# Compact near products in a diagonal scan, C turned by 128 columns, the first output chunk in other banks, and a new slot table

## The reference, cut to what matters

```
h = rms(x); u, z_s5, q, k, v, z_da = split(h @ e_w_in)
# S5: 64 groups of 16 channels, 64 complex states each; per token l:
x_l = Bbar u_l ; h_l = a * h_(l-1) + x_l ; y_l = Re(C h_l) + d * u_l
y = gelu(y); y = y * sigmoid(y @ w_glu + b_glu) * silu(z_s5)
# differential attention, 8 heads with two score maps each, ALiBi, rms of the output
x = x + concat(y_s5, y_da) @ e_w_out
```

## Time and profile before

| | us |
|---|---|
| median of three runs (lowest, highest) | 985.17 (984.67, 985.78) |
| the profiled execution, time | 983.37 |
| the profiled execution, span of the trace | 981.6 |
| DVE busy / ACT busy in the span | 629.2 / 572.5 |
| ACT splitting weights (L942) / DVE splitting weights (L950) | 310.1 / 361.1 |

### The profile page before, as it was taken

One profiled execution on the slowest core, in us unless ns is written; L12 is line 12 of the kernel. 1 busy time (PEld: TensorE's weight loads), 2 busy tenths in 40 slices (PEclk: granted clock), 3 DMA queues, 4 the chain that ended last, 5 costly groups with the idle time before them and its releaser, 6 DMA issues.

```text
span 981.6 us, 14482 instructions
## 1 busy us (share of the span) xinstructions
PE 966.3 (98%) x5315; PEld 828.8 (84%) x5315; DVE 629.2 (64%) x995; ACT 572.5 (58%) x934; POOL 94.4 (10%) x92
## 2 busy tenths in 40 slices
PE   8999999999999999999999999999999999999998
PEld 7988888788787999888888888888888888888887
DVE  5687898898889755665554654555455545555553
ACT  5697758767567655654445465446545654565332
POOL 2101002011021010000002200220022002200000
PEclk9999999999999999999999999999999999999999
DMA  8874444334433447565799985667999956654662
GB/s 287 207 205 151 151 134 135 119 107 129 141 110 117 129 129 264 166 202 188 173 168 175 168 180 166 177 184 151 173 155 175 196 163 177 180 167 151 215 215 86
DMA packets 113858, 163.63 MB, mean 167 GB/s; under 512 B 19221, under 2 KB 54154, under 8 KB 113546
## 3 DMA queue, kind: packets, MB, share of 16 engines
q1 hardware_dynamic: 99504, 159.67, 61.7%
q10 hardware_dynamic: 14298, 3.22, 1.6%
HBM read 160.76 MB, written 2.10 MB: 166 GB/s over the span
## 4 chain that ended last, share of the span: by engine, by line
PE 90%; DVE 5%; ACT 4%; issue 1%; DMA 0%; SPq 0%; ACTq 0%
PE bank L452 22%; PE bank L454 22%; PE bank L453 22%; PE bank L479 4%; PE bank L480 4%; PE bank L481 4%; ACT uz L1054 2%; PE bank L706 1%; PE bank L691 1%; ACT wh L942 1%; DVE wl L950 1%; PE bank L595 1%; PE bank L520 1%; PE bank L586 1%; PE bank L698 1%
## 5 line engine op out<-in xcount | busy, mean ns | idle before, releaser
L950 DVE TENSOR_TENSOR wl<-raw,wh 128x1024 fp32r<-128x1024 f32 x295 | 361.1, 1228 | 273.0 <-ACT wh L942 271.8
L942 ACT ACTIVATE wh<-raw 128x1024 fp32r<-128x1024 f32 x295 | 310.1, 1057 | 170.0 <-PE bank L454 124.6
L452 PE MATMUL bank<-wh,xh 128*128 128x512 f32 x768 | 309.1, 403 | 0.0
L454 PE MATMUL bank<-wh,xl 128*128 128x512 f32 x768 | 300.3, 391 | 0.0
L453 PE MATMUL bank<-wl,xh 128*128 128x512 f32 x768 | 299.2, 390 | 0.0
L454 PEld LDWEIGHTS bank<-wh,xl 128*128 128x128 f32 x768 | 144.1, 188 | 31.7
L453 PEld LDWEIGHTS bank<-wl,xh 128*128 128x128 f32 x768 | 144.7, 188 | 26.9
L452 PEld LDWEIGHTS bank<-wh,xh 128*128 128x128 f32 x768 | 144.5, 188 | 27.0 <-DVE wl L950 0.2
L452 PE MATMUL bank<-wh,yh 128*128 128x512 f32 x256 | 100.7, 393 | 1.4 <-ACT scr L1345 1.4
L454 PE MATMUL bank<-wh,yl 128*128 128x512 f32 x256 | 99.8, 390 | 0.0
L453 PE MATMUL bank<-wl,yh 128*128 128x512 f32 x256 | 99.6, 389 | 0.0
(11 more groups left out here) (326 smaller groups left out, 1107.2 us busy)
## 6 DMA issues: line engine op xcount, KB each, us to landing
raw<-in_o_w_in SPq DMA_DIRECT2D x128, 512.0 KB
raw<-in_e_w_in SPq DMA_DIRECT2D x130, 256.0 KB, 3.2
raw<-in_e_w_out SPq DMA_DIRECT2D x32, 512.0 KB
raw<-in_o_w_out SPq DMA_DIRECT2D x32, 512.0 KB
raw<-in_e_w_in SPq DMA_DIRECT2D x31, 512.0 KB
raw<-in_s_w_glu SPq DMA_DIRECT2D x8, 512.0 KB
res<-in_x SPq DMA_DIRECT2D x8, 256.0 KB, 6.9
res<-in_x SPq DMA_DIRECT2D x1, 2048.0 KB, 10.1
```

The costliest lines, as they stand in the source:

```text
L452: nc.tensor.matmul(o, l_hi, w_hi, start=first, stop=False)
L454: mm = nc.tensor.matmul(o, l_lo, w_hi, start=False, stop=last)
L942: nc.scalar.activation(wh[:, j % RING, :], raw[:, j % RING, :], ACT.Copy).then_inc(hi_done, 1)
L950: nc.vector.tensor_tensor(wl[:, j % RING, :], raw[:, j % RING, :], wh[:, j % RING, :].bitcast(F32), ALU.subtract).then_inc(lo_done, 1)
```

## The change

Five things change, all in layer 0.

1. **Near products.** DVE no longer writes `ca` with its zeros: it writes the compact C-times-powers into `cc` (8 x 5 x 16 columns, all 128 partitions, one instruction instead of two of 64 partitions). PE multiplies `ba` by the 64 compact columns, and the skip term by 16 columns. ACT spreads the result into `near` with eight scaled copies per call (scale 1 or 0 by row group) instead of four, and a new ACT piece `s5_pad` makes the padded `ca` from `cc` with two copies of 64 partitions for each of the two parts; `s5_out_y` waits for it.
2. **C turned by 128 columns.** C is loaded twice into both halves of `c_n` (six matrix loads on ACT's queue instead of four, in six consecutive slots), PE uses four 128-column transposes per call instead of eight 64 x 64 products, one slot earlier, and ACT's `c_out` becomes four calls of two copies.
3. **First output chunk.** It accumulates in `xb` and `yb`, so it no longer waits for the sigmoids; the second now waits for all eight, the fourth for the second chunk's sum. In each of its units ACT and DVE now do the gate pieces ahead of the split of the weights.
4. **Slots.** Nearly all slots of scan and attention move.
5. **Waits.** `rotate_in` and `rotate_out` wait for the near products and the pad; small setup reductions build `ident16` and `of_group`.

```diff
-TAB_SLOT, FAR_SLOT, BA_SLOT = [-2, -2], [-6, -1], [-11, -2]
-T_SLOT = [0, 0, 0, 0]
-NEAR_SLOT, HOLD_SLOT, SKIP_SLOT = [0, 4], 4, -9
-X_SLOT, YN_SLOT, Y_SLOT = [3, 6], 7, [9, 9]
-IN_SLOT, OUT_SLOT = [4, 8], [5, 8]
+TAB_SLOT, FAR_SLOT, BA_SLOT = [0, 0], [-6, -4], [-8, -2]
+T_SLOT = [-1, -1, -1, -1]
+NEAR_SLOT, HOLD_SLOT, SKIP_SLOT = [-1, 1], 6, -11
+X_SLOT, YN_SLOT, Y_SLOT = [0, 5], 3, [8, 9]
+IN_SLOT, OUT_SLOT = [2, 6], [6, 6]
+PAD_SLOT = [-3, 3]
-QKT_SLOT = [-3, -3]
+QKT_SLOT = [-3, -2]
-PV_SLOT = [5, 7]
-YT_SLOT = [10, 11]
-V_SLOT, SILU_SLOT = 4, 5
-SQUARE_SLOT, SUM_SLOT, NORM_SLOT = [9, 10], [8, 10], [10, 13]
+PV_SLOT = [5, 8]
+YT_SLOT = [8, 13]
+V_SLOT, SILU_SLOT = 3, 6
+SQUARE_SLOT, SUM_SLOT, NORM_SLOT = [8, 10], [8, 9], [11, 11]
...
+        out0_acc = [[xb, yb], acc[1], acc[0], acc[1]]
... PE, s5_near
                 if h == 0:
-                    pe.wait_ge(ca_done, i + 1)
+                    pe.wait_ge(cc_done, 2 * i + 2)
                     pe.wait_ge(dd_done, i + 1)
                 for e in range(TH):
-                    t, at = TH * h + e, e * P
-                    nc.tensor.matmul(o[0:32, at:at + P], ba[:, 0, t, 0:32], ca[:, 0, t, 0:P], start=True, stop=False)
-                    nc.tensor.matmul(o[0:32, at:at + P], ba[:, 1, t, 0:32], ca[:, 1, t, 0:P], start=False, stop=False)
-                    mm = nc.tensor.matmul(o[0:32, at:at + 32], ident[:, 32 * e:32 * e + 32],
-                                          diag_d[:, h, 32 * e:32 * e + 32], start=False, stop=True)
+                    t, at = TH * h + e, e * 64
+                    for r in range(2):
+                        nc.tensor.matmul(o[0:32, at:at + 64], ba[:, r, t, 0:32],
+                                         cc[r][:, t, 0:HOP, :].rearrange("p k h -> p (k h)"), start=r == 0, stop=False)
+                    mm = nc.tensor.matmul(o[0:32, at:at + 16], ident[:, 32 * e:32 * e + 32],
+                                          diag_d[:, h, :], start=False, stop=True)
... PE, s5_out_y
+                if h == 0:
+                    pe.wait_ge(ca_done, i + 1)
... PE, c_turn
-                of = ident.rearrange("p (q g h) -> p g q h", q=4, g=2)
-                for g in range(2):
-                    for a in range(CT // 2 * (k % 2), CT // 2 * (k % 2 + 1)):
-                        mm = nc.tensor.matmul(bank[4 + k // 2][64 * g:64 * g + 64, 64 * a:64 * a + 64],
-                                              c_n[:, k // 2, a, :], of[:, g], start=True, stop=True)
+                for e in range(CT // 2):
+                    a = CT // 2 * (k % 2) + e
+                    mm = nc.tensor.transpose(bank[4 + k][:, e * P:(e + 1) * P],
+                                             c_n[:, k // 2, a, :, :].rearrange("p g n -> p (g n)"), ident)
... PE, output chunks
-                if n < 2:
-                    pe.wait_ge(glu_sig, 4 * n + 4)
-                else:
-                    pe.wait_ge(x1_done, 2 * (n - 1))
+                if n:
+                    pe.wait_ge(glu_sig, CT)
+                if n == 3:
+                    pe.wait_ge(x1_done, 4)
... ACT
-                        if j % 2 == 0:
-                            dst, src, arrived = matrices[j // 2]
+                        if j < 6:
+                            dst, src, arrived = matrices[j]
...
+            def c_out(k):
+                act.wait_ge(c_ps_in, k + 1)
+                for g in range(2):
+                    at = slice(64 * g, 64 * g + 64)
+                    src = bank[4 + k][at, :].rearrange("p (b i g h) -> p b i g h", b=2, g=2, h=16)[:, :, :, g, :]
+                    dst = bc_all[at, 2 * (k % 2):2 * (k % 2) + 2, 2 + k // 2, :].rearrange("p b (i h) -> p b i h", h=16)
+                    ins = nc.scalar.activation(dst, src, ACT.Copy, scale=1.0 if k < 2 else -1.0)
+                ins.then_inc(bc_c, 1)
... ACT, s5_near
                 for s in range(HOP):
-                    at = 32 * (HOP - 1 - s)
-                    ins = nc.scalar.activation(near[32 * s:32 * s + 32, TH * h:TH * h + TH, at:P], src[:, :, 0:P - at], ACT.Copy)
+                    dst = near[32 * s:32 * s + 32, TH * h:TH * h + TH, :].rearrange("p i (k g c) -> p i k g c", k=HOP, g=2)
+                    for g in range(2):
+                        ins = nc.scalar.activation(dst[:, :, HOP - 1 - s:HOP, g, :], src[:, :, 0:s + 1, :], ACT.Copy,
+                                                   scale=of_group[0:32, g:g + 1])
+            def s5_pad(i, r):
+                act.wait_ge(cc_done, 2 * i + (r + 1))
+                if r == 0:
+                    act.wait_ge(y_ps, i) if i else act.wait_ge(zeros, 2)
+                for g in range(2):
+                    at = slice(64 * g, 64 * g + 64)
+                    dst = ca[at, r, :, :].rearrange("p i (k h) -> p (i k) h", k=5)[:, :, 16 * g:16 * g + 16]
+                    ins = nc.scalar.activation(dst, cc[r][at].rearrange("p i k h -> p (i k) h"), ACT.Copy)
+                if r:
+                    ins.then_inc(ca_done, 1)
... ACT, output chunks
-                    split_hi(act, CH_OUT0 + n, j + LEAD)
                     if n == 0 and 1 <= j < 5:
                         glu_up(2 * j - 2)
                         glu_up(2 * j - 1)
+                    split_hi(act, CH_OUT0 + n, j + LEAD)
... DVE, s5_far
-                times(ca_t[0], r, 0)
-                link(times(ca_t[1], 1 - r, 1))
-                for half in range(2):
-                    at = slice(64 * half, 64 * half + 64)
-                    o = ca[at, r, :, :].rearrange("p i (k h) -> p (i k) h", k=5)[:, :, 16 * half:16 * half + 16]
-                    ins = v.tensor_tensor(o, *(x[at].rearrange("p i k h -> p (i k) h") for x in ca_t),
-                                          ALU.subtract if r else ALU.add)
+                times(cc[r], r, 0)
+                link(times(ca_t, 1 - r, 1))
+                flat_of = "p i k h -> p (i k h)"
+                v.tensor_tensor(cc[r].rearrange(flat_of), cc[r].rearrange(flat_of), ca_t.rearrange(flat_of),
+                                ALU.subtract if r else ALU.add).then_inc(cc_done, 1)
+                dve.wait_ge(cc_done, 2 * i + (r + 1))
... DVE, output chunks (split_lo moves behind glu_mul and glu_low)
-                    split_lo(dve, CH_OUT0 + n, j + LEAD)
                     if n == 0:
                         if j < 4:
                             glu_mul(2 * j)
...
+                    split_lo(dve, CH_OUT0 + n, j + LEAD)
```

More of the change, by code:

```diff
@@ L209, in build @@
         g_half = small_at(166, 2)
+        quarter = small_at(168, 8)
+        of_group = small_at(176, 2)
+        ident16 = small_at(178, 16)
         qk = carve("scr", NT, CW)
@@ L259, in build @@
         bt = [flat[:, 4096 + 512 * k:4608 + 512 * k].rearrange("p (a h) -> p a h", a=GP) for k in range(2)]
-        ca_t = [flat[:, 3072 + 640 * k:3072 + 640 * (k + 1)].rearrange("p (i k h) -> p i k h", i=TB, k=5)
-                for k in range(2)]
+        ca_t, *cc = [flat[:, at:at + 640].rearrange("p (i k h) -> p i k h", i=TB, k=5) for at in (3072, 3840, 4480)]
         ba_t = [x.rearrange("p r n -> p (r n)").rearrange("p (i s h) -> p i s h", i=TB, s=HOP) for x in prod]
@@ L310, in build @@
         u4_done, slopes = sem("u4_done"), sem("slopes")
-        ba_done, ca_done, dd_done, steps_done = (sem(n) for n in
-            ("ba_done", "ca_done", "dd_done", "steps_done"))
+        ba_done, cc_done, ca_done, dd_done, steps_done, group_done = (sem(n) for n in
+            ("ba_done", "cc_done", "ca_done", "dd_done", "steps_done", "group_done"))
         t_ps, xin_sb, near_ps, near_sb, x_ps, x_read, h_done, y_ps = (sem(n) for n in
@@ L436, in unit_ready, with rows_unit @@
                 pe.wait_ge(lo_done, (c * UNITS) + (j + 1))
-            def rows_unit(c, j, left, kts, pair):
+            def rows_unit(c, j, left, kts, pair, out=None):
                 lh, ll = left
@@ L449, in rows_unit @@
                     first, last = j == 0 and a == 0, j == UNITS - 1 and a == UK - 1
-                    o = acc[pair][t][:, :]
+                    o = (out or acc[pair])[t][:, :]
                     l_hi, l_lo = lh[:, kt, t * P:(t + 1) * P], ll[:, kt, t * P:(t + 1) * P]
@@ L500, in qk_turn @@
                         pe.wait_ge(yt_lo, n)
+                else:
+                    pe.wait_ge(bc_c, 4)
                 o = (trb, yb)[h]
@@ L974, in _ @@
                       enumerate(("da_lambda_q1", "da_lambda_k1", "da_lambda_q2", "da_lambda_k2"))]
-            matrices += [(c_n[:, at, :, :], d[name][0].rearrange("(a b) h p -> (b h) a p", b=8), s5_in)
-                      for at, name in ((0, "s5_c_re"), (1, "s5_c_im"))]
+            matrices += [(c_n[:, at, :, g, :], d[name][0].rearrange("(a b) h p -> (b h) a p", b=8), s5_in)
+                      for at, name in ((0, "s5_c_re"), (1, "s5_c_im")) for g in range(2)]
             def tiles_up(b):
@@ L1011, in chunk_tokens @@
                     ins.then_inc(u4_done, 1)
-            def c_out(r):
-                act.wait_ge(c_ps_in, 2 * r + 2)
```

(16 more changed lines are left out.)

30 lines of the change are left out of this document (14 added, 16 removed).

## The result

| | before | after |
|---|---|---|
| median us | 984.92 (983.63 to 985.78) | 972.12 (970.89 to 973.47) |
| profiled execution, its span | 983.37, 981.6 | 973.47, 971.8 |

The ratio is 0.9872, with a 95% interval of 0.9861 to 0.9884: 12.6 us faster, 11.4 to 13.7. The prediction, 971.8 in a range of 968.0 to 979.5, holds it. The sum, however, comes out right because errors in it nearly cancel: a charge that did not come and a gain sized too low on the one side, a wait that I missed on the other. The traces show them.

The account below looks back on a forecast made before the run. PE was taken as the bound, busy for 966.3 of the 981.6 us span. Terms of 6.9 + 1.8 + 1.6 + 3.4 + 0.7 - 1.0 = 13.4 us took the median from 985.17 to 971.8 us, 8-in-10 range 968.0 to 979.5.

Parts of the forecast that it names:

- near products: PE's scan: with 64 moving columns at 0.056 us each, a call falls from 2.00 to 1.14 us; eight calls win 6.9.
- C turn on PE: Four calls of 0.90 us become four of four transposes, 0.44 each; wins 1.8 us.
- first output chunk: After GLU's last product on PE: the chunk no longer waits for sigmoids; wins 1.6 us.
- transposes' stretch: From first transpose to near products: all four batches fall to 2.63 us; wins 3.4, range 0 to 6.
- scores' wait: PE's wait at the scores, from DVE's split and `score_in` behind `s5_far`, goes; wins 0.7 us.
- new waits in the slots: Attention and scan slots: late fourth score product and the slot where both scans meet, charged -1.0 us for four batches.
- the loads, two more and closer together: Two more 256 KB DMAs on ACT's queue: data lands in time, so hidden; costs nothing, up to 1 us for the range.
- rival C: DVE becomes the bound, slower than before, 991 at 7 us late; signs include weight units waiting; chance 0.06.
- Place (c): Slots 2 and 3: ACT's near copies delay the second exponential, `combine` and `score_in`; fourth score product 0.2 to 0.3 us late per batch.
- The slots' term: New slot table for scan and attention: wins 3.4 us at the transposes and 0.7 at the scores, 4.1 in all.

Follow-up runs that it names:

- e7_near_twice: The kernel of e1_spaced with every near product done twice, the second overwriting the first; 977.72 us, ratio 0.9925.
- e3_old_turn: The changed kernel with the C turn of before and its four spaced matrix loads; 971.40 us, ratio 0.9869.
- e1_spaced: The changed kernel with its six matrix loads issued in slots 0, 2, 4, 5, 6, 7 instead of 0 to 5; 969.40 us, ratio 0.9843.
- e4_old_banks: The changed kernel with the first output chunk back in acc[0] and the old waits on the sigmoids; 974.20 us, ratio 0.9890.
- e6_new_slots_before: The kernel before with only the slot table of the changed kernel; 980.04 us, ratio 0.9949.
- e2_dense_before: The kernel before with its four matrix loads issued in slots 0 to 3 instead of 0, 2, 4, 6; 986.06 us, ratio 1.0020.
- e5_old_slots: The kernel of e1_spaced with the slot table of before for scan and attention, pad in slots -3 and 3; 982.99 us, ratio 0.9980.
- e9_third_bank: The kernel of e1_spaced with the third transpose block in an idle bank and the first near products ahead of the fourth block; 967.41 us, ratio 0.9826.

## Why the prediction was right, and where it was not

Its steps, with what the profile's starts and the experiments say:

| step | forecast | measured |
|---|---|---|
| near products | 6.9 | 7.0 (8 x 0.87); price confirmed by e7_near_twice |
| C turn on PE | 1.8 | 2.6 (e3_old_turn against e1_spaced: 2.6) |
| first output chunk | 1.6 | 1.6 (e4_old_banks: 1.8) |
| transposes' stretch | 3.4 | 3.4 (2.62 or 2.63 in all four) |
| scores' wait | 0.7 | 0.7 |
| new waits in the slots | -1.0 | 0 |
| the loads, two more and closer together | 0, up to -1 | -4.3 in the profile, -2.9 by the medians (e1_spaced) |

Without the last line the measured terms come to 15.3, and the profiles of before and e1_spaced differ by 922.5 - 907.0 = 15.5 from the first attention step on: nothing of size is missing from the list.

**Right.** What was to be won lay in PE's stream and in the wait that the list names wrongly. Reading starts instead of the list's idle times gave 3.4 us where the first two scan lines of the earlier trace rows, 5.2 us in sum, mix what goes with the ping-pong that stays. That `s5_far` was the late one fits e6_new_slots_before, where only the table changed and the stretch fell to 2.63; the table moves other pieces too, so it does not single `s5_far` out. No rival of the prediction happened, but one of the signs that I had named for rival C did, weight units waiting for the low part, from a cause that no rival held.

**Wrong: the loads.** The step that failed is "hidden" for the two more DMAs, priced at nothing. I asked when the data would land (10.7 us) and what it would take from the weight loads, and never what the issue itself costs the engine that makes it. The row was at hand in the trace of before: an issue of 1.96 us in that stretch, and 0.96 us of ACT idle for it. Six issues in six slots made two of them 4.25 and 8.65 us long, and ACT's splits behind them late; three units of lead did not cover that. e1_spaced and e2_dense_before settle it from both sides. It was not the two loads more that cost, but the slot lost between the B loads and the first C load, to which the prediction gave no price.

**Wrong the other way: the charge of 1.0 and the C turn.** Place (c), the fourth score product, has no wait, although the near copies cost more than I said: 2.68 us from the start of a call's eight to their end, not 2.35. The group rows, 297 to 456 ns and 3.0 in sum, overlap a little; for the same columns they are some 80 ns above the old ones (350 against 267 for 128). The new copies have a scale per partition and write runs of 16 columns; which of the two costs the 80 ns was not measured apart. The pad, with such runs and no scale, cost 0.73 each against 0.69. My slot count was pessimistic by at least 0.3 us per batch there. For the C turn I counted 0.44 of transposes against 0.90; the four take 0.35, and by the starts the slot with them shrinks from 3.85 to 3.19 us, since the unit behind takes 2.84 instead of 2.95. The two errors together gave 1.8 us, the missed wait took 2.9 by the medians; the rest is the spread of the runs. That these nearly cancel is luck. Set against the profiled execution, where the wait was 4.3 us, the forecast of 970.0 was 3.5 us short.

**The slots' term** of 4.1 was right for the old code (5.0 in e6_new_slots_before), but it isn't what the slots are worth in the change. Taken away from it, they cost 13.5 (e5_old_slots). The parts aren't additive: with the old slots the C turn and the first output chunk (4.2 by starts) are worth more than the 2.0 us that e5_old_slots saves in all, so there the new near products with their pad and copies cost some 2 us instead of saving 7. A term measured on one side only would have misled.

## What to carry to other kernels

Before adding DMAs to a compute engine's queue or moving them closer together, look at how long the issues there already take, and which of them are long: here leaving a slot between the B loads, and between them and the load behind, was enough. The issue blocks the engine, and the splits behind it pay. Read starts, not the idle column, when a wait is to be priced, and look for a flag that ends just ahead of the start, as the engine named may have been done long before. Compare two profiles from a landmark behind the start, not by their spans. Price a new slot table with the new code and with the old, since work per slot and place of the slot pay off together.

## What the runs showed of the hardware

- An issue of a 256 KB load on ACT's queue took 0.39 us with no large load ahead of it, 4.25 to 8.65 us right behind one of the B loads (after, e2_dense_before, e4_old_banks), 1.19 to 2.44 us two slots behind one, and 0.37 to 2.04 us behind a C load. Once the work started beside it was done, ACT stood still until the issue was through (3.19 and 7.71 us idle).
- The granted clock fell to 0.50 for some 3 to 7 us in the profiles of the kernels with the old slots and the compact near products, with PE busy for 2.25 of 4.24 us ahead of it in the one case, and came back under dense products. The fall cost 2.0 us there (e5_old_slots), and it does not come in every execution of the same kernel (7 of 12). No window of 2 us between 60 and 400 us shows less than 1.00 in the profiles of before, after, e1_spaced, e6_new_slots_before and e9_third_bank.
- A product with 64 moving columns took 0.056 to 0.058 us per instruction with 32 stationary columns (e7_near_twice), 0.056 with 64, and 0.107 with 128.
